# Key pages of a paged cache: one transfer of whole rows in place of two transfers of half rows

## The chip, the cores and the metric

The kernel runs on one core of a Trainium2 chip. The metric is the device time of one execution in microseconds; a lower one is better. The time before is the median of three runs.

## What is computed

One inference step of one decoder layer, for a prompt of 256 tokens and for 8 sample sequences with one new token each, all in f32. The part that the change touches is the attention of the 8 samples over their paged past of 2048 keys, 16 pages of 128 keys, found through a page table:

```
k_past = cache_k[l][page_table].reshape(bs, n_pages * PAGE_SIZE, N_HEADS, 2, HEAD_DIM)
v_past = cache_v[l][page_table].reshape(bs, n_pages * PAGE_SIZE, N_HEADS, V_DIM)

def diff_attention(q, k, v, q_pos, k_pos, rel_bias, lam):
    s = jnp.einsum('bqhjd,bkhjd->bhjqk', q, k) * (HEAD_DIM ** -0.5)
    ...
    p = jax.nn.softmax(s, axis=-1)
    p_diff = p[:, :, 0] - lam * p[:, :, 1]
    return jnp.einsum('bhqk,bkhe->bqhe', p_diff, v)
```

With 8 heads, two maps per head and 64 columns each, a key has 1024 values (4 KB); a page of 128 keys is 512 KB. Around it lie an input projection (`x @ w_in`), the same attention for the prompt, a complex diagonal state-space layer with GELU and a gate, two branch projections, an output projection, a gated MLP with a causal convolution, and two layer norms.

## The kernel before

The program is written out engine by engine, with semaphores. It has two parts. In the first, up to about 760 us, TensorE (PE) makes the 72 output tiles of the input projection and of the GLU as f32 products with weight tiles that stream through a ring (L708), and between them, at places counted in products (`z_groups` with its hooks `at`), does the small products of everything else. In the second part each weight tile is split by ACT (L1431) and DVE (L1899) into a high and a low part, and PE makes three products per tile (L1030, L1031, L1036).

The sample attention runs beside the projection, one sequence after the other: keys of sequence b+1 while the values of sequence b are used. For the keys:

- SyncE (SP) loads a page into `k_pages`, a ring of four pages. `load_keys` (L434) reads the page number from SBUF (`value_load`, L436), then for each half e of the row (512 of the 1024 columns) waits until that half of the slot is free and issues a transfer of 128 x 512 (L438, L439).
- GpSimd (POOL) multiplies a half in place by the query row that is broadcast to all partitions (`products`, L620; L627), after it waited for that half's transfer.
- VectorE (DVE) sums the products over the 64 columns of each map (`reduce_page`, L1728; L1735) into `score` and counts the half as free in `k_free`.

Pages are numbered n = 16 b + p, halves 2n + e; a half of the ring is used again every 8 halves, so half 2n + e waits for `k_free` at 2n + e - 7.

For the values, `load_values` (L442) waits until PE has used the page four before (`v_used`) and then calls `load_page` (L428), which reads the page number (L430) and issues one transfer of 128 x 1024 (L431). PE's product with it is `page_pv` (L681, L688).

All of these loads stand in one hand-written order on SP, which executes in order. For each of the seven turns of its loop (L471) it is

```
for what in ("K4", "Sk", "P14", "P15", "V0", "K5", "V1", "K6", "Sv", "V2", "K7", "V3", "K8", "Q", "V4", "K9",
             "V5", "K10", "V6", "K11", "V7", "V8", "K12", "V9", "K13", "V10", "K14", "V11", "K15", "V12",
             "N0", "N1", "V13", "N2", "N3"):
```

K is a key page of sequence i+1, N one of sequence i+2, V a value page of sequence i, P one of sequence i-1, Q the query row, Sk and Sv are stores of new keys and values. A load that waits holds back everything behind it.

POOL also executes in order, and it does a second task between the products: `fractions` (L616, L618), a step of the rotation tables of the state-space layer. In sequence 0 they stand before pages 4 and 8, later before pages 3, 5, 8 and 11. ACT makes their input (`turns`, L1213) and takes their output (`rotation`, L1220 to L1224), DVE uses the tables in `states` (L1679 to L1692), and PE waits for those states in `cx` (L797). DVE executes `states`, the reductions and the softmax of the prompt heads (`maxima`, `differences`) in one fixed order, given in the loop at L1797. The transfers of the weights are issued by ACT, on a queue of its own.

Of the kernel before, what the change touches and what calls it, by code (L numbers as in the profile page):

```python
# [27 lines left out]
PAGES = 16  # L28
POOL_PAGES = 160
KW = H * 2 * HD  # L30
# [50 lines left out]
def wait(eng, sem, value):  # L81

    if isinstance(value, int) and value <= 0:
        return
    eng.wait_ge(sem, value)
# [67 lines left out]
def build(nc, a, out, scratch):  # L153
    with ExitStack() as ctx:
        def sb(name, cols, dt=F32, rows=P):
            return ctx.enter_context(nc.sbuf_tensor(name, [rows, cols], dt))
# [18 lines left out]
        page_no = sb("page_numbers", B * PAGES, I32, rows=1)  # L175
# [3 lines left out]
        def overlay(*parts):  # L179
            with ExitStack() as stage:  # L180
                placed = [stage.enter_context(nc.sbuf_tensor(name, [P, cols], F32)) for name, cols in parts]
            return [t for t, (name, _) in zip(placed, parts) if not name.startswith("skip")]
# [31 lines left out]
        k_pages = work[:, 35288:39384]  # L214
# [57 lines left out]
        def half_page(n):  # L272
            return k_pages[:, n % 8 * KW // 2:(n % 8 + 1) * KW // 2]
# [19 lines left out]
        def sems(*names):  # L293
            return [sem(n) for n in names]
# [6 lines left out]
        k_in = sems(*(f"k_in{j}" for j in range(8)))  # L301
# [25 lines left out]
        kq_ready, k_free = sems("kq_ready", "k_pages_reduced")  # L327
# [37 lines left out]
        def _(sp):  # L365
# [56 lines left out]
            ck = a["cache_k"][0].rearrange("n p h j d -> n p (h j d)")  # L422
            cv = a["cache_v"][0].rearrange("n p h e -> n p (h e)")

            def cache_half(e):
                return ck[:, :, e * KW // 2:(e + 1) * KW // 2]

            def load_page(cache, ring4, arrived, b, p):  # L428
                n = PAGES * b + p
                at = sp.value_load(page_no[0:1, n:n + 1], min_val=0, max_val=POOL_PAGES - 1)  # L430
                sp.dma_start(page(ring4, n), cache[bass.ds(at, 1)].rearrange("o p k -> (o p) k")  # L431
                             ).then_inc(arrived[n % 4], 16)

            def load_keys(b, p):  # L434
                n = PAGES * b + p
                at = sp.value_load(page_no[0:1, n:n + 1], min_val=0, max_val=POOL_PAGES - 1)  # L436
                for e in range(2):
                    wait(sp, k_free, 2 * n + e - 7)  # L438
                    sp.dma_start(half_page(2 * n + e),  # L439
                                 cache_half(e)[bass.ds(at, 1)].rearrange("o p k -> (o p) k")).then_inc(k_in[(2 * n + e) % 8], 16)  # L440

            def load_values(b, p):  # L442
                wait(sp, v_used, PAGES * b + p - 3)
# [13 lines left out]
            for p in range(4):  # L457
                load_keys(0, p)
# [6 lines left out]
            for p in range(4, PAGES):  # L465
                load_keys(0, p)
            for p in range(4):
                load_values(0, p)
            for p in range(4):
                load_keys(1, p)  # L470
            for i in range(H - 1):  # L471
# [3 lines that stand above are left out]
                    kind, p = what[0], int(what[1:]) if what[1:].isdigit() else 0  # L475
# [117 lines left out]
        @block.gpsimd  # L593
        def _(pool):
            ch = Chain(pool, pool_c)
            ch.did(pool.memset(ident[:, :], 0.0))
            ch.wait()
            pool.affine_select(out=ident[:, :], in_=ident[:, :], compare_op=ALU.not_equal, fill=1.0, base=0,
                               pattern=[[-1, P]], channel_multiplier=1).then_inc(const_ready, 1)
            pool.memset(small[0:NB + 1, 32:32 + H], MASK).then_inc(rel_ready, 1)  # L600
            for tensor, value in ((ones[:, :], 1.0), (mean_w[:, :], 1.0 / D), (v_mean_w[:, :], 1.0 / P),
                                  (small[:, 4:5], PI / 2), (small[:, 5:6], EPS), (small[:, 6:7], 4 * EPS)):
                pool.memset(tensor, value).then_inc(const_ready, 1)

            times_i = score[0][:, 0:T].bitcast(I32)
            ch.did(pool.iota(times_i, pattern=[[1, T]], base=1, channel_multiplier=0))
            ch.wait()
            pool.tensor_copy(times, times_i).then_inc(times_ready, 1)
            pool.memset(b_pad[:, :], 0.0).then_inc(bpad_zero, 1)
            pool.memset(MT[:, :, 256:512], 0.0).then_inc(mt_zero, 1)  # L610

            def fractions(n):

                turns, whole_turns, part = (tab[n % 2][:, k * 256:(k + 1) * 256] for k in range(3))
                pool.wait_ge(tv_ready, n + 1)
                ch.did(pool.tensor_scalar(whole_turns, turns, 1.5 * 2 ** 23, -1.5 * 2 ** 23, ALU.add, ALU.add))  # L616
                ch.wait()
                pool.tensor_tensor(part, turns, whole_turns, ALU.subtract).then_inc(tf_ready, 1)  # L618

            def products(b, p):  # L620

                n = PAGES * b + p
                if p == 0:
                    pool.wait_ge(qb_in[b % 2], 16 * (b // 2 + 1))
                for e in range(2):
                    pool.wait_ge(k_in[(2 * n + e) % 8], 16 * (n // 4 + 1))
                    pool.tensor_tensor(half_page(2 * n + e), half_page(2 * n + e), q_b[b % 2][:, e * 512:(e + 1) * 512],  # L627
                                       ALU.mult).then_inc(kq_ready, 1)

            fractions(0)  # L630
            fractions(1)
            for p in range(PAGES):
                if p == 4:
                    fractions(2)
                if p == 8:
                    fractions(3)
                products(0, p)
            fractions(4)
            fractions(5)
            for i in range(H):  # L640
                for p in range(PAGES if i + 1 < B else 0):
                    if p == 3:
                        fractions(4 * i + 6)
                    if p == 5:
                        fractions(4 * i + 7)
                    if p == 8 and i + 2 < HT:
                        fractions(4 * i + 8)
                    if p == 11 and i + 2 < HT:
                        fractions(4 * i + 9)
                    products(i + 1, p)  # L650

            def centre(ln):

                pool.wait_ge(mean_copied, ln + 1)
                for g in (0, 1):
                    c3 = x3[:, 4 * g:4 * g + 4, :]
                    pool.tensor_tensor(c3, c3, mean_y.unsqueeze(1).to_broadcast([P, 4, N]), ALU.subtract  # L657
                                       ).then_inc(cent_ready, 1)

            centre(0)  # L660
            centre(1)
# [3 lines left out]
        def _(pe):  # L665
# [356 lines left out]
            def products(m, off, sums):  # L1022


                pe.wait_ge(wh_ready, m + 1)
                for dst, k0, highs, lows, start, _, ready in sums:
                    for k in range(len(highs)):
                        if ready is not None:
                            pe.wait_ge(*ready(k))
                        pe.matmul(dst[:, 0:N], weight(w_hi, off, k0 + k), highs[k], start=start and k == 0, stop=False)  # L1030
                        last = pe.matmul(dst[:, 0:N], weight(w_hi, off, k0 + k), lows[k], start=False, stop=False)  # L1031
                last.then_inc(wh_used, 1)
                pe.wait_ge(wl_ready, m + 1)
                for dst, k0, highs, _, _, stop, _ in sums:
                    for k in range(len(highs)):
                        last = pe.matmul(dst[:, 0:N], weight(w_lo, off, k0 + k), highs[k], start=False,  # L1036
                                         stop=stop and k == len(highs) - 1)
                last.then_inc(slot_done, 1)
# [1069 lines left out]
```

## Time and profile before

| | us |
|---|---|
| median of 3 runs | 1740.39 |
| lowest and highest | 1736.45, 1743.41 |
| profiled execution, its own time | 1737.55 |
| its span, first to last instruction | 1735.6 |
| busy: PE / DVE / ACT / POOL | 1660.1 / 1121.9 / 651.6 / 391.2 |
| mean clock granted to TensorE, share of full | 0.979 |
| read from HBM, written | 385.47 MB, 7.02 MB |

The sum of an engine's busy time says how full it is, not what ends the program. The stages have different limits: before 760 us transfers, POOL, DVE and PE hand work to each other, after it PE works nearly without a gap. In the rows below "idle" in brackets is the time in which the engine stood before the instruction, and behind the arrow is the work that released it. SPq is SyncE's own queue of instructions; its DMA rows show when a transfer is issued, and "DMA to landing" how long it took from there. L numbers are lines of the kernel before.

### The profile page before, as it was taken

The numbers are of one execution on the slowest core, as the hardware profiler recorded it, in microseconds if no ns is written. First come the engines' busy times: TensorE is split into PE (matmuls) and PEld (weight loads), VectorE is DVE, ScalarE is ACT, GpSimd is POOL, SyncE is SP. The second block draws the span as 40 slices with busy tenths as digits, with TensorE's granted clock in tenths as the row PEclk, the third lists the DMA queues.
The fourth block names the chain that finished last, engine by engine and source line by source line (L and its number), as shares of the span: only waits on it lengthen the run. The fifth ranks groups of instructions, "written<-read, shape, count | busy, mean of one in ns | idle before, by whom it ended". The sixth has DMA issues, their size and how long they took to land. (4 is left out here: it accounts for less than half of the span.)

```text
span 1735.6 us, 31618 instructions
## 1 busy us (share of the span) xinstructions
PE 1660.1 (96%) x11736; PEld 1473.4 (85%) x11736; DVE 1121.9 (65%) x1740; ACT 651.6 (38%) x986; POOL 391.2 (23%) x341
## 2 busy tenths in 40 slices
PE   7996999999999999989997999999999999999997
PEld 5884876666677667789997999999999999999996
DVE  1345487878878764567667767777777776555555
ACT  2021134434334322333335544444444444333333
POOL 1044576766866860000001000000000000000001
PEclk9898999999999999999998999999999999999998
DMA  9775899999999996776664557667667675766651
GB/s 224 169 228 169 274 325 368 361 376 384 362 379 378 367 344 213 225 195 177 183 182 121 158 160 209 176 174 195 163 184 188 169 190 143 211 175 181 178 163 51
DMA packets 502962, 393.63 MB, mean 227 GB/s; under 512 B 25439, under 2 KB 451316, under 8 KB 502548
## 3 DMA queue, kind: packets, MB, share of 16 engines
q1 hardware_dynamic: 419908, 325.07, 62.2%
q10 hardware_dynamic: 82944, 67.11, 12.3%
q8 instruction: 67, 1.10, 0.3%
q14 instruction: 43, 0.34, 0.1%
HBM read 385.47 MB, written 7.02 MB: 226 GB/s over the span
## 5 line engine op out<-in xcount | busy, mean ns | idle before, releaser
L708 PE MATMUL bank<-work,weight_ring 128*128 128x264 f32 x2176 | 522.5, 396 | 0.5 <-ACT work L1152 0.5
L1431 ACT ACTIVATE weights_hi<-weight_ring 128x2048 fp32r<-128x2048 f32 (+1 forms) x166 | 309.7, 1866 | 514.6 <-PE bank L1031 386.8
L708 PEld LDWEIGHTS bank<-work,weight_ring 128*128 128x128 f32 x2176 | 412.5, 194 | 94.8 <-issue 25.1
L1899 DVE TENSOR_TENSOR weights_lo<-weight_ring,weights_hi 128x2048 fp32r<-128x2048 f32 (+1 forms) x166 | 369.1, 2224 | 112.6 <-ACT weights_hi L1431 67.5
L627 POOL TENSOR_TENSOR work<-work 128x512 f32<-128x512 f32 x256 | 318.7, 1277 | 95.6 <-DMA work<-in_cache_k 73.9
L1030 PE MATMUL bank<-h_hi,weights_hi 128*128 128x264 f32 x1344 | 331.0, 284 | 0.0
L1031 PE MATMUL bank<-h_lo,weights_hi 128*128 128x264 f32 x1344 | 330.2, 284 | 0.0
L1030 PEld LDWEIGHTS bank<-h_hi,weights_hi 128*128 128x128 f32 x1344 | 253.2, 188 | 0.0
L1031 PEld LDWEIGHTS bank<-h_lo,weights_hi 128*128 128x128 f32 x1344 | 252.7, 188 | 0.0
L657 POOL TENSOR_TENSOR work<-work,ffn_scratch 128x1056 f32<-128x1056 f32 x4 | 9.5, 2407 | 1058.4 <-ACT ffn_scratch L1152 1058.4
L1735 DVE TENSOR_REDUCE work<-work 128x8 f32<-128x512 f32 x256 | 164.5, 677 | 47.8 <-POOL work L627 47.5
L1036 PE MATMUL bank<-h_hi,weights_lo 128*128 128x264 f32 x1344 | 176.5, 284 | 0.0
L1030 PE MATMUL bank<-hidden_hi,weights_hi 128*128 128x264 f32 x688 | 169.7, 284 | 1.8 <-DVE ffn_scratch L2027 1.8
L1031 PE MATMUL bank<-hidden_lo,weights_hi 128*128 128x264 f32 x688 | 169.3, 284 | 0.0
L1036 PEld LDWEIGHTS bank<-h_hi,weights_lo 128*128 128x128 f32 x1344 | 168.4, 188 | 0.0
L1152 ACT ACTIVATE work<-bank 128x256 f32<-128x256 f32 (+8 forms) x124 | 43.0, 357 | 305.2 <-PE bank L708 135.2
L1030 PEld LDWEIGHTS bank<-hidden_hi,weights_hi 128*128 128x128 f32 x688 | 129.5, 188 | 2.0 <-DVE ffn_scratch L2027 2.0
L1031 PEld LDWEIGHTS bank<-hidden_lo,weights_hi 128*128 128x128 f32 x688 | 129.4, 188 | 0.0
L2024 DVE SCALAR_TENSOR_TENSOR ffn_scratch<-bank,conv_and_ln_parameters,ffn_scratch 128x255 f32<-128x255 f32 x86 | 41.5, 483 | 128.0 <-ACT ffn_scratch L1152 128.0
L1036 PE MATMUL bank<-hidden_hi,weights_lo 128*128 128x264 f32 x688 | 91.3, 284 | 0.0
L1036 PEld LDWEIGHTS bank<-hidden_hi,weights_lo 128*128 128x128 f32 x688 | 86.7, 188 | 0.0
L688 PE MATMUL bank<-work 128*16 128x256 f32 x1024 | 71.0, 384 | 14.7 <-DMA work<-in_cache_v 13.9
(269 smaller groups left out, 1911.9 us busy)
## 6 DMA issues: line engine op xcount, KB each, us to landing
weight_ring<-in_w_up SPq DMA_DIRECT2D x86, 1024.0 KB, 5.7
work<-in_cache_k SPq DMA_DIRECT2D x256, 256.0 KB, 5.9
work<-in_cache_v SPq DMA_DIRECT2D x128, 512.0 KB, 6.1
weight_ring<-in_w_in ACTq DMA_DIRECT2D x60, 1024.0 KB, 11.5
weight_ring<-in_w_down SPq DMA_DIRECT2D x32, 1024.0 KB, 6.0
weight_ring<-in_w_out SPq DMA_DIRECT2D x16, 1024.0 KB, 6.0
weight_ring<-in_w_down SPq DMA_DIRECT2D x16, 704.0 KB, 4.9
weight_ring<-in_w_proj_attn SPq DMA_DIRECT2D x16, 512.0 KB, 4.2
```

Of the source, the lines that this page charges most:

```text
L627: pool.tensor_tensor(half_page(2 * n + e), half_page(2 * n + e), q_b[b % 2][:, e * 512:(e + 1) * 512], ALU.mult).then_inc(kq_ready, 1)
L657: pool.tensor_tensor(c3, c3, mean_y.unsqueeze(1).to_broadcast([P, 4, N]), ALU.subtract).then_inc(cent_ready, 1)
L688: last = pe.matmul(bank[5][32 * g:32 * g + 16, 0:2 * P], score[b % 3][:, p * 16:(p + 1) * 16], page(v_pages, n)[:, g * 2 * P:(g + 1) * 2 * ...
L708: last = pe.matmul(bank[(n + m) % 2][:, 0:N], chunk_weight(g, k - c * per, m), tiles[k], start=(k == 0), stop=(k == len(tiles) - 1))
L1030: pe.matmul(dst[:, 0:N], weight(w_hi, off, k0 + k), highs[k], start=start and k == 0, stop=False)
L1031: last = pe.matmul(dst[:, 0:N], weight(w_hi, off, k0 + k), lows[k], start=False, stop=False)
L1036: last = pe.matmul(dst[:, 0:N], weight(w_lo, off, k0 + k), highs[k], start=False, stop=stop and k == len(highs) - 1)
L1152: return act.activation(dst, src, ACT.Copy, scale=scale)
L1431: act.activation(w_hi[:, (j % 2) * KT * P:(j % 2) * KT * P + k_tiles * P].bitcast(F32R), slot3(j, 0, k_tiles).rearrange("p k m -> p (k m)" ...
L1735: dve.tensor_reduce(score[b % 3][:, p * 16 + 8 * e:p * 16 + 8 * e + 8], half_page(2 * n + e).rearrange("p (m d) -> p m d", d=HD), AX.X, AL ...
L1899: dve.tensor_tensor(w_lo[:, cols].bitcast(F32R), slot3(off % SLOTS, 0, k_tiles).rearrange("p k m -> p (k m)"), w_hi[:, cols], ALU.subtract ...
L2024: n1 = ch.did(dve.scalar_tensor_tensor(y[:, 1:T], ps[:, 0:T - 1], par(1), y[:, 1:T], ALU.mult, ALU.add))
```

## The change

`load_keys` now issues one transfer of 128 x 1024, by the same `load_page` as the values. It waits for both halves of the slot. The wait stands before the call, and so before the page number is read. POOL waits once per page, for the whole of it; its two products, DVE's two reductions and the two counts in `k_free` stay as they are. Of the eight semaphores `k_in` four are used.

```diff
@@ -422,9 +422,6 @@
             ck = a["cache_k"][0].rearrange("n p h j d -> n p (h j d)")
             cv = a["cache_v"][0].rearrange("n p h e -> n p (h e)")
 
-            def cache_half(e):
-                return ck[:, :, e * KW // 2:(e + 1) * KW // 2]
-
             def load_page(cache, ring4, arrived, b, p):
                 n = PAGES * b + p
                 at = sp.value_load(page_no[0:1, n:n + 1], min_val=0, max_val=POOL_PAGES - 1)
@@ -432,12 +429,8 @@
                              ).then_inc(arrived[n % 4], 16)
 
             def load_keys(b, p):
-                n = PAGES * b + p
-                at = sp.value_load(page_no[0:1, n:n + 1], min_val=0, max_val=POOL_PAGES - 1)
-                for e in range(2):
-                    wait(sp, k_free, 2 * n + e - 7)
-                    sp.dma_start(half_page(2 * n + e),
-                                 cache_half(e)[bass.ds(at, 1)].rearrange("o p k -> (o p) k")).then_inc(k_in[(2 * n + e) % 8], 16)
+                wait(sp, k_free, 2 * (PAGES * b + p) - 6)
+                load_page(ck, k_pages, k_in, b, p)
 
             def load_values(b, p):
                 wait(sp, v_used, PAGES * b + p - 3)
@@ -622,8 +615,8 @@
                 n = PAGES * b + p
                 if p == 0:
                     pool.wait_ge(qb_in[b % 2], 16 * (b // 2 + 1))
+                pool.wait_ge(k_in[n % 4], 16 * (n // 4 + 1))
                 for e in range(2):
-                    pool.wait_ge(k_in[(2 * n + e) % 8], 16 * (n // 4 + 1))
                     pool.tensor_tensor(half_page(2 * n + e), half_page(2 * n + e), q_b[b % 2][:, e * 512:(e + 1) * 512],
                                        ALU.mult).then_inc(kq_ready, 1)
```

Line numbers behind the first piece move up by 7 in the changed kernel; L427 and L428 there are L430 and L431 here.

On SP, at the key page "K4" of the second turn of the loop, the store behind it and the two value pages P14 and P15, the rows before are these (k_pages_reduced is `k_free`, v_pages_used is `v_used`; the ISA rows are register work):

```order
L436 TENSOR_LOAD page_numbers
L436 ISA x2
L439 ISA [waits k_pages_reduced]
L439 DMA work<-in_cache_k 128x512
L439 ISA [waits k_pages_reduced]
L439 DMA work<-in_cache_k 128x512
L452 DMA out_k_prompt<-work 128x2x128 [waits mail_read]
L430 TENSOR_LOAD page_numbers [waits v_pages_used]
L430 ISA x2
L431 ISA
L431 DMA work<-in_cache_v 128x1024
```

The same place in the changed kernel:

```order
L427 TENSOR_LOAD page_numbers [waits k_pages_reduced]
L427 ISA x2
L428 ISA
L428 DMA work<-in_cache_k 128x1024
L445 DMA out_k_prompt<-work 128x2x128 [waits mail_read]
L427 TENSOR_LOAD page_numbers [waits v_pages_used]
L427 ISA x2
L428 ISA
L428 DMA work<-in_cache_v 128x1024
```

One transfer and one wait are gone per key page, and the wait has moved from the register work behind the load of the page number to that load itself.

On POOL, at the first pages of sequence 0, before:

```order
L627 TENSOR_TENSOR work<-work 128x512 [waits k_in0,q_broadcast_in0]
L627 TENSOR_TENSOR work<-work 128x512 [waits k_in1]
L627 TENSOR_TENSOR work<-work 128x512 [waits k_in2]
L627 TENSOR_TENSOR work<-work 128x512 [waits k_in3]
L627 TENSOR_TENSOR work<-work 128x512 [waits k_in4]
```

And in the changed kernel:

```order
L620 TENSOR_TENSOR work<-work 128x512 [waits k_in0,q_broadcast_in0]
L620 TENSOR_TENSOR work<-work 128x512
L620 TENSOR_TENSOR work<-work 128x512 [waits k_in1]
L620 TENSOR_TENSOR work<-work 128x512
L620 TENSOR_TENSOR work<-work 128x512 [waits k_in2]
```

No product moved; each second one no longer waits for a transfer of its own.

## Rows read from the trace of the kernel before

**Rows 1.** The page, part 2: clock granted to TensorE in 40 slices, tenths of full.
```profile
PEclk9898999999999999999998999999999999999998
```

**Rows 2.** Stages: us, busy (count) of PE PEld DVE ACT POOL, PEclk, DMA, GB/s.
```profile
240.00:640.00 400.00, 383.74 (x2361) 273.25 (x2360) 319.94 (x533) 156.24 (x336) 292.06 (x249) 1.00 1.03 370
...
760.00:1735.00 975.00, 951.26 (x7714) 944.30 (x7713) 644.14 (x934) 415.64 (x479) 9.55 (x4) 0.99 0.63 170
```

**Rows 3.** Waits, whole run: who <- for whom: us in total, times, longest.
```profile
POOL work L627 <- DMA work<-in_cache_k: 73.9, 28, 15.3
...
PE bank L797 <- DVE conv_and_ln_parameters L1692: 16.2, 1, 16.2
...
PE bank L688 <- DMA work<-in_cache_v: 13.9, 15, 2.6
```

**Rows 4.** Timeline around the first long wait: start us, us, what, [idle <-releaser].
```profile
143.02 1.25 DVE L1735 TENSOR_REDUCE work<-work 128x8 f32<-128x512 f32 x2
...
143.86 0.92 SPq L439 DMA_DIRECT2D work<-in_cache_k  x2
...
146.25 2.46 DVE L1735 TENSOR_REDUCE work<-work 128x8 f32<-128x512 f32 x4
...
147.25 7.52 POOL L627 TENSOR_TENSOR work<-work 128x512 f32<-128x512 f32 x6 [15.32 <-DMA work<-in_cache_k]
...
164.98 1.91 PE L797 MATMUL bank<-conv_and_ln_parameters,work 128*32 128x256 f32 x4 [16.25 <-DVE conv_and_ln_parameters L1692]
```

**Rows 5.** Timeline of one turn of the loop (head 4).
```profile
437.07 1.07 POOL L616 TENSOR_SCALAR work<-work 128x256 f32<-128x256 f32 x1 [10.48 <-ACT work L1213]
...
448.12 19.93 POOL L627 TENSOR_TENSOR work<-work 128x512 f32<-128x512 f32 x16
...
467.11 1.25 DVE L1735 TENSOR_REDUCE work<-work 128x8 f32<-128x512 f32 x2
...
470.10 2.54 SPq L431 DMA_DIRECT2D work<-in_cache_v  x3
...
476.67 0.63 PE L688 MATMUL bank<-work 128*16 128x256 f32 x8 [0.94 <-DMA work<-in_cache_v]
```

**Rows 6.** PE's timeline, waits on value pages.
```profile
281.86 0.63 PE L688 MATMUL bank<-work 128*16 128x256 f32 x8 [1.45 <-DMA work<-in_cache_v]
283.11 1.05 PE L688 MATMUL bank<-work 128*16 128x256 f32 x8 [0.63 <-DMA work<-in_cache_v]
...
515.10 0.62 PE L688 MATMUL bank<-work 128*16 128x256 f32 x8 [1.42 <-DMA work<-in_cache_v]
...
605.94 0.63 PE L688 MATMUL bank<-work 128*16 128x256 f32 x8 [0.17 <-DMA work<-in_cache_v]
...
636.55 0.62 PE L688 MATMUL bank<-work 128*16 128x256 f32 x8 [1.21 <-DMA work<-in_cache_v]
```

**Rows 7.** Lines L430 and L431 (value pages), then L439 in 140:152 (half key pages).
```profile
L430 SPq TENSOR_LOAD <-page_numbers x128: 262/269/717, 177.0 to 712.2; - x128
...
L431 SPq DMA_DIRECT2D work<-in_cache_v x128: 332/333/615, 177.7 to 712.9; - x128
...
DMA to landing us min/median/max: 3.3/6.1/10.5
...
DMA to landing us min/median/max: 2.6/3.3/3.6
```

**Rows 8.** SP at page 79, L439 in 451.8:452.8, and POOL at page 31.
```profile
451.86 0.85 SPq L439 DMA_DIRECT2D work<-in_cache_k  x2
...
DMA to landing us min/median/max: 5.4/5.4/5.5
...
264.16 6.44 POOL L627 TENSOR_TENSOR work<-work 128x512 f32<-128x512 f32 x5 [0.45 <-DMA work<-in_cache_k]
```

**Rows 9.** Busy time in two short stretches, with PEclk; columns as above.
```profile
165.00:170.00 5.00, 5.00 (x11) 3.03 (x12) 5.00 (x10) 0.00 (x0) 4.15 (x4) 0.50 0.56 172
...
283.00:286.00 3.00, 2.89 (x12) 1.66 (x13) 2.90 (x6) 1.01 (x3) 1.58 (x2) 0.50 1.03 370
```


## The prediction

> **What bounds the kernel now.** I read the page first. TensorE's granted clock is 0.8 or more of full in every slice, mostly 0.9 or more [rows 1], so its time is work or waits, and only a little throttling. The table by stage adds that in 240 to 640 us PE works 383.7 of 400 us while the 16 DMA engines are full (share 1.03); after 760 us PE works 951 of 975 us and no key page is left [rows 2]. So what the change can move lies before 760 us, and there PE has little idle time. The waits name it [rows 3]: one wait of 16.2 us on the state chain (DVE L1692), and 13.9 us in 15 waits on value pages. PE never waits on a key page. GpSimd (POOL) does, for 73.9 us in 28 waits; SyncE (SP), which issues the loads, waits for DVE to free half pages before it. The question is which of these two lead to PE.
>
> The 16.2 us wait does. POOL reaches page 5 and stands until 147.25, since SP could issue that page only at 143.86, when DVE had reduced the halves of page 1. POOL then does six products, pages 5 to 7, in 7.52 us, and only behind them its fraction step L616. From it go the tables on ACT, the states on DVE and the product on PE (164.98 us) [rows 4]. Each us by which page 7's products end later is a us of PE.
>
> The value waits lead there too, by a loop of one turn per head, shown for one head [rows 5]: PE ends a tile, ACT evicts it and makes the next turns, POOL is released by them (437.07) and does 16 products in a row from 448.12, DVE reduces behind it up to page 79, and after its other work page 80 (467.11); SP, which had stood at the next key page, goes on through a store to value pages (470.10), and PE gets the second of them at 476.67 after a wait. PE waits at this place in each of six heads, from 2.1 us in the first (281.86 and 283.11) to 0.2 us in the last (605.94) [rows 6], and never runs into slack: the loop goes through PE and turns as slowly as its slowest way. The waits at page 9 of a sequence (such as 1.42 us at 515.10 [rows 6]) lie inside the same turn, so a longer one is taken back at the next place.
>
> **The change, part by part.** (1) The release. Before, the page number was read and the register work done ahead of the wait, and the transfer left 0.17 us after the reduction (DVE's first half of page 1 ends about 143.69, issue at 143.86 [rows 4]). Now the wait stands on the load of the page number, with all of that behind it. A value page already has this form: three of them in a row take 2.54 us [rows 5], 0.33 us of it the last issue itself [rows 7], so they start 1.10 us apart and 0.77 us lie between wait and issue; the load alone is 0.27 us [rows 7]. A key page therefore leaves 0.6 us later than its second half did, and 1.1 to 1.2 us later than its first. Behind it on SP stand the value pages, which leave 0.6 us later wherever SP had been waiting.
>
> The Trainium skill (DMA: Bandwidth & Descriptors, Latency and other measured facts) gives about 600 ns as the floor of such a load. The 0.27 us of the trace decides; with 0.6 the step would be 0.33 us longer in each of the eight places below, 2.6 us in all.
>
> (2) The landing. Halves landed in 2.6 to 3.6 us in the quiet stretch around 147 us; whole 512 KB value pages took 3.3 us at least, 6.1 in the median [rows 7]. In that quiet stretch I take 3.3 for a whole key page, the value page's shortest and the middle of the halves'; 3.0 and 4.0 are the ends. In the full stretch a pair of halves took 5.4 to 5.5 [rows 8], so beside a value page's 6.1 the size counts for a few tenths.
>
> (3) The start. Page 1's second reduction ended about 144.3, so page 5 is issued at 145.05 and lands at 148.35. Page 2 is reduced by 147.5 (two of the four from 146.25 [rows 4]): page 6 issued at 148.3, landed 151.6; its two products end at 154.1 (1.25 each), those of page 7 at 156.6, where they ended at 154.77. **+1.8 us**, between 1.2 and 2.5. The clock stands at 0.50 (1.2 GHz) for the first 5 us after PE resumed [rows 9]. A later start may shorten or lengthen that tail by half of a few us; I take 0, bounds -1 and +2.
>
> (4) The loop, in six heads. The key page that stands ahead of the value pages leaves 0.6 us later: **+3.6 us**. Inside the turn POOL can also wait for pages 14 and 15. At head 4 it took page 79 at 448.12 + 8 x 1.246 = 458.1; the halves, issued at 451.86 and 452.38, landed in 5.4 to 5.5 us, the last at 457.9 [rows 8]. Slack 0.2 against a page 0.3 to 0.6 later: +0.4. At head 1 POOL already waited 0.45 for page 31 [rows 8], so there the full 0.9 counts. Nearly all other rows of POOL in the turn run on without such a wait. Mean 0.5, bounds 0 and 1: **+3.0 us**, 0 to 6. The wait of 1.21 us at 636.55, in the last turn [rows 6], has a key page ahead of its value page on SP: **+0.6 us**.
>
> (5) What is saved. One DMA issue per page (the starts of the pair at 451.86 are 0.85 - 0.33 = 0.52 us apart [rows 8]). Where SP was waiting this saves nothing; where it was not, value pages leave 0.5 us earlier, but those have 1 to 8 us of room. 128 transfers fewer on full engines: bounds 0 and -3 us (at most 0.2 us for each of two landings in the loop, in seven turns), and I take **-1 us**, near the end at 0, since a landing hardly depends on size. POOL's wait count falls by one in two, which has no price: its products follow at 1.25 us in either form. The reductions and their releases stay.
>
> Sum: 1.8 + 3.6 + 3.0 + 0.6 - 1 = **+8 us**. The profiled execution took 1737.55 us, so 1745.6, say **1746 us**. The median of the three runs is 1740.39, 2.8 us above that execution, and they spread over 7 us, so 1748 by the median; about 0.5% (8.7 us) is what a measurement can tell from no change here. The forecast lies just inside it.
>
> **The rivals.**
> *Hidden.* Only the start pays, because the loop has some room that the trace doesn't show (DVE or ACT may wait somewhere in the turn for work that is not on it): +2 us, 1740. For it: the turn's waits are short, 0.2 to 2.1 us [rows 6]. Against it: they come back in six heads of six.
>
> *The key ring becomes the bound (slower).* The place is POOL's run over pages 8 to 15. A slot now turns in two products 2.49, the last reduction 0.68, release 0.77 and a landing L, 3.94 + L; POOL needs 9.97 us for four pages. It decides from L = 6.0 us on, and the median of a value page is 6.1 [rows 7]. At L = 7.0 each four pages cost 1 us, two fours per turn and six turns 12 us more: 1758. Against it: landings are longest when the queue also holds pages that can leave earlier now.
>
> *The clock.* After the two waits at 281.86 and 283.11 (1.45 and 0.63 us) the clock stood at 0.50 for 283 to 286 us [rows 6, 9], a loss of 1.5 us. If longer waits bring this on at the other five turns: +7.5 us, 1753. Against it: the single wait of 1.42 us at 515.10 did not.
>
> *Larger transfers pay (faster).* If whole rows shorten the landings so much that the value pages come in time, at most all 13.9 us of these waits go: 1724, and half of it would be 1731. For it: DMA is full in this stretch. Against it: the waits come from when SP issues, not from bandwidth alone; at 470.10 the value pages leave 1.7 us after the reduction of page 80 (467.11 + 1.25) let SP go on [rows 5], and there the bandwidth has no say.
>
> For that rival speaks the Trainium skill (DMA: Bandwidth & Descriptors, Bandwidth), which wants transfers batched and measures 138 GB/s at 64 KB against 341 at 1 MB. No run here compares sizes alone; the two landings above speak against much of it.
>
> **How the numbers follow.** Forecast (+5 to +11 us) 0.50, hidden 0.20, key ring 0.12, clock 0.10, larger transfers 0.08. Of the forecast's 0.50 about 0.15 lies above 8.7 us; with the ring and most of the clock case slower has 0.36. Faster has half of the last case, 0.04; the rest is 0.60. The range leaves out the gain and the far ends of ring and clock: 1739 to 1759 us.
>
> **What would show it.** Right: the first wait of PE on L1692 grows from 16.2 to about 18 us; key issues come 0.77 us after the reduction; the value waits grow from 13.9 us to some 17 to 21; POOL's waits on keys grow in the loop; all after 760 us stays. Wrong: value waits below 13.9 us, a first wait that is not longer, POOL idle before most pages (the ring), or new stretches at clock 0.50.

## The result, and the profile after

| | before | after |
|---|---|---|
| median of 17 runs, us | 1739.8 | 1745.72 |
| lowest and highest, us | 1733.49, 1743.41 | 1740.59, 1751.69 (one more at 3306.83) |
| span of the profiled execution, us | 1735.6 | 1742.0 |
| clock granted to TensorE | 0.979 | 0.98 |
| POOL's waits on key pages | 73.9 in 28 | 81.6 in 44 |
| PE's waits on value pages | 13.9 in 15 | 19.9 in 19 |
| PE's wait on the state chain | 16.2 | 18.4 |

The ratio is 1.0041, with an interval of 1.0028 to 1.0054: slower by 0.4%, a difference of 5.9 us in the medians. One execution of 3306.83 us stands apart and is left out of the ratio. Runs of the changed kernel beside later experiments gave 1.0054 [1.0033 to 1.0074] again.

The page of the changed kernel, its clock, the queue and the issues:

```profile
PEclk9997999999999999999998999999999999999998
...
q1 hardware_dynamic: 401476, 325.07, 62.0%
...
work<-in_cache_k SPq DMA_DIRECT2D x128, 512.0 KB, 6.1
work<-in_cache_v SPq DMA_DIRECT2D x128, 512.0 KB, 6.2
```

The clock row is that of before but for two slices near the start [rows 1]. Half the transfers of keys, twice as large, land 6.1 us after their issue in the median. On the page of the kernel before, the same two rows are these:

```profile
q1 hardware_dynamic: 419908, 325.07, 62.2%
...
work<-in_cache_k SPq DMA_DIRECT2D x256, 256.0 KB, 5.9
```

So the bytes are the same, the time that they take on the 16 DMA engines is the same (62.0 against 62.2%), and one whole row lands about as late after its issue as one half did.

The stages of the changed kernel (columns as in rows 2):

```profile
240.00:640.00 400.00, 378.99 (x2317) 270.07 (x2316) 316.36 (x521) 156.17 (x336) 289.16 (x246) 1.00 1.01 364
760.00:1742.00 982.00, 956.54 (x7765) 950.07 (x7763) 648.91 (x941) 417.43 (x480) 9.54 (x4) 0.99 0.64 171
```

In 240 to 640 us PE is busy for 4.75 us less than before, with the DMA share still at full. The waits (as in rows 3):

```profile
POOL work L620 <- DMA work<-in_cache_k: 81.6, 44, 16.5
...
PE bank L681 <- DMA work<-in_cache_v: 19.9, 19, 1.7
PE bank L790 <- DVE conv_and_ln_parameters L1685: 18.4, 1, 18.4
```

PE's two waits grew by 2.2 and 6.0 us. The timeline around the first of them, to be read against [rows 4]:

```profile
141.34 1.25 DVE L1728 TENSOR_REDUCE work<-work 128x8 f32<-128x512 f32 x2
...
143.35 5.16 SPq L428 DMA_DIRECT2D work<-in_cache_k  x3
...
146.69 2.48 POOL L620 TENSOR_TENSOR work<-work 128x512 f32<-128x512 f32 x2 [16.53 <-DMA work<-in_cache_k]
...
165.44 1.91 PE L790 MATMUL bank<-conv_and_ln_parameters,work 128*32 128x256 f32 x4 [18.39 <-DVE conv_and_ln_parameters L1685]
```

DVE ends the second half of page 1 at 142.59, the transfer of page 5 leaves at 143.35, 0.76 us later, and POOL begins 3.34 us after that. Between pages POOL now stands too (the piece of 1.14 us before page 6 is in its 44 waits); before, all six products ran in one piece.

Where the time went follows from the start of the same instruction in both executions. PE's first products on the last of the 16 value pages, at the ends of the first three turns and of the sixth; the last row is page 7 of the seventh sequence, inside the last turn:

```profile
283.74 0.62 PE L681 MATMUL bank<-work 128*16 128x256 f32 x8 [1.10 <-DMA work<-in_cache_v]
...
349.44 0.62 PE L681 MATMUL bank<-work 128*16 128x256 f32 x8 [1.33 <-DMA work<-in_cache_v]
...
415.47 0.84 PE L681 MATMUL bank<-work 128*16 128x256 f32 x8 [1.26 <-DMA work<-in_cache_v]
...
612.14 0.62 PE L681 MATMUL bank<-work 128*16 128x256 f32 x8 [1.07 <-DMA work<-in_cache_v]
...
642.51 0.63 PE L681 MATMUL bank<-work 128*16 128x256 f32 x8 [0.96 <-DMA work<-in_cache_v]
```

- Up to the small products of `cx` that start at 106.88 us (108.56 before) the changed kernel is 1.68 us ahead. Nothing of the change acts there; a stretch at half clock was shorter in this execution (last section).
- From there to the end of the first long wait: 165.44 against 164.98, so 2.14 us lost.
- To the last page of the first turn: 283.74 against 283.11, 0.17 us more.
- From there to the last page of the sixth: 328.40 against 322.83 us (605.94 - 283.11 [rows 6]), 5.57 us lost.
- On to page 7 in the last turn, 642.51: 30.37 against 30.61 us, nothing lost; and the second part begins at 752.84 against 746.79, the end comes at 1742.0 against 1735.6. Nothing happens behind 760 us.

### The profile page after: what moved, and what is told of

The parts are those of the page before. It is cut to its first block and busy times, and to the rows that moved or that the text cites. A ratio compares the mean times of both kernels' runs of the same rounds, so it can differ in the third digit from the quotient of the medians.

```text
span 1742.0 us, 31234 instructions
## 1 busy us (share of the span) xinstructions
PE 1657.2 (95%) x11736; PEld 1471.8 (84%) x11736; DVE 1124.6 (65%) x1740; ACT 651.3 (37%) x986; POOL 391.8 (22%) x341
## 5 line engine op out<-in xcount | busy, mean ns | idle before, releaser
L620 POOL TENSOR_TENSOR work<-work 128x512 f32<-128x512 f32 x256 | 319.3, 1276 | 103.1 <-DMA work<-in_cache_k 81.6
L681 PE MATMUL bank<-work 128*16 128x256 f32 x1024 | 70.6, 383 | 20.5 <-DMA work<-in_cache_v 19.9
```

Of the source, the lines that this page charges most:

```text
L681: last = pe.matmul(bank[5][32 * g:32 * g + 16, 0:2 * P], score[b % 3][:, p * 16:(p + 1) * 16], page(v_pages, n)[:, g * 2 * P:(g + 1) * 2 * ...
```

## The experiments

Ratios are to the kernel before, run on the same chip in the same series. e1, e2, e3 and e4 shared one chip, e0, e5, e7 and e9 a second, e1 again, e7 again and e8 a third.

**The page number read ahead of the wait, whole rows kept (e1).**

```diff
 def load_keys(b, p):
-    wait(sp, k_free, 2 * (PAGES * b + p) - 6)
-    load_page(ck, k_pages, k_in, b, p)
+    n = PAGES * b + p
+    at = sp.value_load(page_no[0:1, n:n + 1], min_val=0, max_val=POOL_PAGES - 1)
+    wait(sp, k_free, 2 * n - 6)
+    sp.dma_start(page(k_pages, n), ck[bass.ds(at, 1)].rearrange("o p k -> (o p) k")
+                 ).then_inc(k_in[n % 4], 16)
```

> The changed kernel, with the page number read before the wait for the slot and only the transfer behind it. My theory prices the register load behind the wait at 0.6 us in each of the two release steps of the start and in each turn of the loop, 3.6 of the 6.1 us that the loop lost and 0.6 of the start. Expected: key issues 0.17 us after the reduction again; the first wait of PE about 17.8 us instead of 18.4; value waits near 16 us instead of 19.9; the time 3 to 4 us below the changed kernel, 1741.5 to 1743 (ratio to before 1.001 to 1.002). Rival one, the whole transfer and POOL's wait for all of it carry the cost: the time stays at 1744 to 1746. Rival two, the landing of larger transfers: the same, 1744 to 1746.

Measured: 1736.42 us, ratio 0.9994 [0.9976 to 1.0011], and a second time 1736.81, 0.9992 [0.9974 to 1.001]. The whole loss is gone, more than was expected.

> The changed kernel with the page number read before the key wait, again, to narrow its interval. By the theory that the load behind the wait is the whole cost of the loop, only the start's 1.3 us remain and SP saves an issue per page: ratio 0.999 to 1.001. If it lies at 1.002 or above, whole transfers cost something by themselves.

Its timeline:

```profile
140.74 1.25 DVE L1731 TENSOR_REDUCE work<-work 128x8 f32<-128x512 f32 x2
142.18 4.75 SPq L435 DMA_DIRECT2D work<-in_cache_k  x3
...
145.77 2.48 POOL L623 TENSOR_TENSOR work<-work 128x512 f32<-128x512 f32 x2 [15.82 <-DMA work<-in_cache_k]
```

Its waits:

```profile
POOL work L623 <- DMA work<-in_cache_k: 72.7, 34, 15.8
...
PE bank L684 <- DMA work<-in_cache_v: 14.3, 15, 2.1
PE bank L793 <- DVE conv_and_ln_parameters L1688: 17.6, 1, 17.6
```

From the end of the reduction (141.99) to the issue it is 0.19 us, not 0.76. The value waits are back at 14.3, against 13.9 before and 19.9 after. The first wait stays 1.4 us above that of before: in the quiet stretch the late release of the first half and the landing of the whole row remain, and e2 below has 0.6 of the 1.4 us.

**Halves kept, the first half released as late as the second (e2).**

```diff
 for e in range(2):
-    wait(sp, k_free, 2 * n + e - 7)
+    wait(sp, k_free, 2 * n - 6)
```

> The kernel before, with one constant changed: the first half of a key page waits, like the second, until both halves of the slot are free. Two transfers of half rows, the number read first, POOL waiting per half. Both halves leave 0.6 us and 0.5 us later than before, and the value pages behind them 0.5 us later. Expected by my theory (what counts is when SP goes on behind the key page, and when the last half lands): start +0.6 to +1.1 us, loop +0.5 us a turn, so +3 to +4.5 us, 1743 to 1744.5 (ratio 1.002 to 1.0025). Rival, only whole pages and larger transfers cost: ratio 1.000, 1740. Against the run with the number first it tells what one transfer in place of two is worth with the same wait.

Measured: 1741.16 us, 1.0016 [0.9996 to 1.0036]. The middle is a little below what was expected, and no change lies in the interval too, so alone it decides nothing. Beside e1 it does more. Both read the number first and wait for the same count, and they differ in halves against whole rows only: 0.9994 and 0.9992 against 1.0016, about 4 us for the whole rows. Single runs of the two overlap; the means of the twelve runs of each on one chip differ by 4.2 us, with an interval of 1 to 7. In e2's trace PE's first wait is 16.8 us and the value waits are 18.7, in e1's 17.6 and 14.3: whole rows cost a little in the start and give more back in the loop.

**Two more loads behind the wait (e9).** Their results are not used.

```diff
 def load_keys(b, p):
     wait(sp, k_free, 2 * (PAGES * b + p) - 6)
+    n = PAGES * b + p
+    for _ in range(2):
+        sp.value_load(page_no[0:1, n:n + 1], min_val=0, max_val=POOL_PAGES - 1)
     load_page(ck, k_pages, k_in, b, p)
```

> The changed kernel with two more loads of the page number (results unused) between the wait for the slot and the transfer of a key page: the suspected cost tripled, by about 1.1 to 1.2 us a page. If the load behind the wait is what the change costs, through the first stall once and through the turn of each head, the time rises by another 9 to 14 us over the changed kernel (start +1.1, six turns +1.2 to +1.9 each, the last turn +1), ratio to before 1.009 to 1.012; PE's first wait 19.3 to 19.6 us, value waits 27 us or more. Rival, the transfers or POOL's whole-page wait carry the cost and SP has room: under 3 us more, ratio below 1.006.

Measured: 1765.08 us, 1.0158 [1.0138 to 1.0177], beside 1745.17 for the changed kernel in the same series (e0). That is more than expected.

> The changed kernel as it is, on the same chip as the others of this call, so that they can be compared with it directly. Expected by every theory: ratio to before 1.003 to 1.005.

In e9 the reduction of page 1 ends at 142.44 and the issue comes 1.85 us later; the timeline, from POOL's row at 460.06 on in the turn of head 4:

```profile
144.29 5.75 SPq L428 DMA_DIRECT2D work<-in_cache_k  x3
...
460.06 2.49 POOL L623 TENSOR_TENSOR work<-work 128x512 f32<-128x512 f32 x2 [0.41 <-DMA work<-in_cache_k]
462.90 2.50 POOL L623 TENSOR_TENSOR work<-work 128x512 f32<-128x512 f32 x2 [0.34 <-DMA work<-in_cache_k]
466.66 5.26 POOL L623 TENSOR_TENSOR work<-work 128x512 f32<-128x512 f32 x4 [1.26 <-DMA work<-in_cache_k]
474.38 2.50 POOL L623 TENSOR_TENSOR work<-work 128x512 f32<-128x512 f32 x2 [2.46 <-DMA work<-in_cache_k]
```

Its waits:

```profile
POOL work L623 <- DMA work<-in_cache_k: 124.3, 73, 16.4
...
PE bank L684 <- DMA work<-in_cache_v: 29.6, 23, 3.6
```

POOL stands before 73 of the 128 pages, where it stood before 44 in the changed kernel: here the ring of keys has become a bound, as in the rival of that name. In the changed kernel it hardly has. The same run of pages there:

```profile
452.75 12.58 POOL L620 TENSOR_TENSOR work<-work 128x512 f32<-128x512 f32 x10
...
465.49 2.67 POOL L620 TENSOR_TENSOR work<-work 128x512 f32<-128x512 f32 x2 [0.17 <-DMA work<-in_cache_k]
...
468.96 2.49 POOL L620 TENSOR_TENSOR work<-work 128x512 f32<-128x512 f32 x2 [0.80 <-DMA work<-in_cache_k]
471.66 2.50 POOL L620 TENSOR_TENSOR work<-work 128x512 f32<-128x512 f32 x2 [0.21 <-DMA work<-in_cache_k]
```

Ten of the sixteen products run without a stop, then three short waits, where before all sixteen ran in one piece [rows 5]. With e1 there are three points: issue 0.19, 0.76 and 1.85 us behind the reduction, ratio 0.9993, 1.0048 (the middle of 1.0041 and 1.0054) and 1.0158. The first step costs 9.6 us for 0.57 us, the second 19 us for 1.09 us: 17 us of time for each us of delay, in both.

That is not the price of the delay alone. The mean granted clock over all runs is 0.980 in e1, 0.979 in the changed kernel and 0.974 in e9. The share not granted, times the span, is 35, 38 and 45 us. By this estimate, which counts every such us as lost, up to 3 us of the first step and up to 8 us of the second are clock. Without them each us of delay costs 10 to 12 us.

**Value pages ahead of the key pages at two places on SP (e3), and the same in the kernel before (e4).**

```diff
-                for what in ("K4", "Sk", "P14", "P15", "V0", ...
+                for what in ("P14", "P15", "K4", "Sk", "V0", ...
...
-                             ... "V7", "V8", "K12", "V9", "K13", ...
+                             ... "V7", "V8", "V9", "K12", "K13", ...
```

> The changed kernel with another order on SP: value pages 14 and 15 stand ahead of the key page 4 of the next sequence, value page 9 ahead of key page 12. These value pages no longer stand behind a key page that waits for DVE. By my theory the value waits of PE at these places (about 17 of 19.9 us) go, and with them the loop: the time falls by 12 to 17 us to 1729 to 1734. Only the start's 2 us of the change then remain against the same order of the kernel before. Rival, POOL or the key ring bounds the turn: PE waits for ACT, DVE or other value pages instead, and the time falls by under 5 us.

> The kernel before with the same new order on SP (value pages 14 and 15 ahead of key page 4, value page 9 ahead of key page 12). My theory: some 10 of the 13.9 us of value waits go, the time falls by 8 to 11 us to 1729 to 1732, and the changed kernel in this order is only about 2 us slower than this one. Rival, the change costs its 6 us on another way than through the value pages: the two stay 6 us apart.

Measured: e3 1724.81 us, 0.9924 [0.9902 to 0.9946]; e4 1726.3, 0.9929 [0.9904 to 0.9955]. Both gain more than expected, and the two can't be told apart. The value waits of e3, then of e4:

```profile
PE bank L681 <- DMA work<-in_cache_v: 2.8, 5, 0.9
```

```profile
PE bank L688 <- DMA work<-in_cache_v: 7.6, 6, 2.6
```

In this order the changed kernel is no longer measurably the slower one. So its loss in the loop went through the value pages that stood behind a waiting key page. The gain of the new order (12 us on the kernel before, 20 us on the changed one) shows also what this order costs before any change.

**The fraction step of sequence 0 before page 5 instead of page 8 (e5, on the changed kernel).**

```diff
-                if p == 8:
+                if p == 5:
                     fractions(3)
```

> The changed kernel with one step moved on POOL: the fraction step that stood before the products of page 8 of sequence 0 now stands before those of page 5, where POOL waits for a transfer anyway. If the first wait of PE (18.4 us) is the chain page 5 landed, six products, fraction step, tables, states, it shrinks to 6 to 8 us, since DVE can begin the states at its last reduction (about 149 us) and not at 160; the time falls by 9 to 12 us against the changed kernel to 1733 to 1736 (a shorter stretch at the lower clock may add 1 to 3 us). Rival, the states wait for something else (ACT's table or DVE's reductions of page 4): under 3 us.

Measured: 1735.18 us, 0.9989 [0.9976 to 1.0002], 10 us below e0. The wait and what ends it:

```profile
146.15 2.48 POOL L620 TENSOR_TENSOR work<-work 128x512 f32<-128x512 f32 x2 [8.31 <-DMA work<-in_cache_k]
...
153.06 1.92 PE L790 MATMUL bank<-conv_and_ln_parameters,work 128*32 128x256 f32 x4 [6.61 <-DVE conv_and_ln_parameters L1685]
```

The step now fills a part of POOL's own wait for page 5, and PE resumes at 153.06 instead of 165.44. This shows the first chain as the prediction read it: key pages 5 to 7 lead to PE's longest wait through POOL's fixed order. By the estimate used above for e9, up to 4 of the 10 us are clock.

**All together, with the change (e7) and without it (e8).** e7 is the changed kernel with the edits of e1, e3 and e5, and values too read their number ahead of the wait; e8 is the kernel before with the order of e3, the step of e5 and the same for values.

> The changed kernel with all that the theory says helps: number read before the wait for keys and for values, value pages 14, 15 and 9 ahead of the key pages that wait, fraction step before page 5. The new SP order alone gave 1724.8 on the changed kernel. Adding the other two: 9 to 12 us from the first stall, 1 to 3 us from the remaining value waits and the 0.6 us of release. Expected 1711 to 1715 (ratio 0.984 to 0.987), faster than both kernels. Rival, the gains overlap and another wait takes their place: 1718 or more.

> The kernel before with everything of the run with all together except the change itself: halves as before, new order on SP, fraction step before page 5, number read before the wait for values too. It tells whether whole-row transfers are worth anything once nothing waits behind them. My theory: 128 fewer issues on SP let the value pages that still wait (page 5 and page 13 of a sequence, 7.6 us in the half-row kernel with the new order against 2.8 us in the whole-row one) leave earlier, so this kernel is 2 to 6 us slower than the whole-row one: 1711 to 1715, ratio 0.985 to 0.988. Rival, whole rows are worth nothing or cost the first half's delay: this kernel is equal or faster, ratio 0.982 to 0.984.

> The run with all together, again, on the same chip as its half-row counterpart for a direct comparison. Expected by every theory: ratio 0.982 to 0.986.

Measured: e7 1708.96 us, 0.9836 [0.9813 to 0.9859], and again 1713.06, 0.9856 [0.9827 to 0.9886]; e8 1718.21, 0.9886 [0.9857 to 0.9915]. e8 lies 3 us above what was expected. On one chip e7 is 5.2 us faster than e8, and of its six runs one reaches into the range of e8's six (1717.35 against a lowest of 1716.14); the intervals overlap a little. PE's value waits are 7.5 us in e8's trace and 2.2 in that of e7 again. So whole rows are worth some 0.3% in this order, with the number read first. e7 is 1.4 to 1.6% faster than the kernel before, and 2.1% faster than the changed kernel beside it (e0).

## Why the prediction came out right, step by step

The forecast was 1746 us and the median 1745.72; the case that it named, a late release that reaches PE by two ways, is the one that the runs show. The steps, against the two traces:

- *The release* (0.77 us after the reduction): 0.76. *The landing* (3.3 us in the quiet stretch): POOL begins after 3.34.
- *The start*, +1.8 us: 2.14. Behind page 5 POOL waited 1.14 us more, for page 6.
- *The loop*, +3.6 + 3.0 - 1, so +5.6 us: 0.17 + 5.57 = 5.74 up to the last page of the sixth turn.
- *The last turn*, +0.6 us: not there. The wait is 0.96 us, less than the 1.21 of before [rows 6], and the stretch up to it takes 0.24 us less.
- The gross sum is 8.1 us; the span grew by 6.4, since this execution came to 106.88 us 1.7 us early. The forecast, +8 on one execution, was a little above the difference of the medians, 5.9 us, and of the 7.1 us that the ratio makes of 1739.8.

**The mechanism and the sum are right, but two parts behind the sum were off, and cancel; that it hit the median within 1 us is luck.** e1 splits the change in two:

- The load behind the wait (e1 to after): 0.0048 to 0.0061, 8 to 11 us. The prediction had 3.6 + 0.6 us for it ahead of the value pages, some 0.6 us in the start, and a share of the 3.0 us for pages 14 and 15, so 5 to 8 us.
- All the rest, whole rows with the number read first (before to e1): ratios of 0.9994 and 0.9992, some 1 us gained, which can't be told from 0. The prediction had what is left of its sum, 0 to 3 us lost.

e2 splits the rest once more: 0.0016 or 2.8 us from before to e2, which its interval doesn't tell from 0, and 4.0 us back from e2 to e1. These 4 us do not measure the term *What is saved* (-1, with a bound of -3). In e2 the second half is issued some 0.5 us behind the first, and both behind the release; a whole row leaves with the first. In the kernel before, where SP is waiting, the second half leaves at its own release: for page 5 at 144.45 (143.86 + 0.92 - 0.33 [rows 4, 7]), 0.18 us after the second reduction (143.02 + 1.25 [rows 4]), and the whole row of e1 leaves 0.19 us after it. So against the kernel before, "where SP was waiting this saves nothing" stands, and e1 gains back for the larger part what e2 had lost. In 240 to 640 us the median from issue to landing is 6.3 us for e1's whole rows and 6.0 for e2's halves, so in e1 a page is complete 0.2 us earlier and SP goes on 0.5 us earlier. That this is the way of the 4 us is argued; no run took it away alone.

The term of the load was sized as eight places (the start, six turns, the last turn) and a mean of 0.5 us at a second place in each of six. The 10 to 12 us per us measured without the clock are near that; the 17 with it are what two places in each of seven turns and the start would make, 15. So what was too small is the clock, which the prediction took at 0 and for the start alone, or the second place. The second can be POOL's waits for pages 14 and 15 (bound 6 us, taken at 3), or PE's waits inside a turn, at page 9 for most, which the prediction took as paid back at the turn's end. In the two traces the 6.0 us more of value waits are 4.2 at the ends of the six turns (5.1 to 9.3 us) and 1.8 inside them (7.6 to 9.4); the wait at page 9 of the fourth sequence that PE uses is one of these, first before, then after:

```profile
450.29 0.62 PE L688 MATMUL bank<-work 128*16 128x256 f32 x8 [0.79 <-DMA work<-in_cache_v]
```

```profile
455.64 0.62 PE L681 MATMUL bank<-work 128*16 128x256 f32 x8 [1.52 <-DMA work<-in_cache_v]
```

So they were not paid back in full. e3 moved the value pages of both places in one run, so how much of the cost belongs to each stays open.

The rivals. *Hidden*: fell, the value waits were longer in each of the first five turns, by 0.5 to 2.1 us, and 0.2 us shorter in the sixth and in the last. *The key ring*: not yet as forecast, but it is what happens with two more loads; POOL's waits went from 28 to 44 and, in e9, to 73. Its point of decision was right in kind: landings of 6.3 us in the full stretch lie just above the 6.0 that were named, and POOL waits 0.2 to 0.8 us before three pages of the turn. *The clock*: in the two profiled executions the loop has one short stretch below full before [rows 9] and one after, so nothing of the difference between these two. Over all runs it is a small part: the mean granted clock was 0.9784 in 16 runs of the changed kernel and 0.9793 in 57 of the kernel before, by estimate 1 to 2 us of the 6. The stretch after:

```profile
415.00:420.00 5.00, 4.53 (x19) 3.15 (x19) 4.90 (x9) 2.32 (x4) 3.49 (x5) 0.66 1.00 383
```

In e9, with waits up to 3.6 us, there are four such stretches (at 384, 459, 487 and 521 us, clock 0.53 to 0.66 over 5 us), so it is a part of what e9 cost. *Larger transfers pay*: not through bandwidth, the queue's share stayed at 62.0%. Whole rows paid 4 us beside e2 and 5 us beside e8, but beside the kernel before itself e1 shows no gain that can be told from 0, and the change as it was made spends 8 to 11 us on the load.

The Trainium skill (DMA: Bandwidth & Descriptors, Bandwidth) wants transfers batched and measures, for transfers issued from GpSimd, 138 GB/s at 64 KB against 341 at 1 MB. The full stretch moved 370 GB/s with halves [rows 2] and 364 with whole rows, so from 256 KB up no gain of that kind is left here. The Trainium skill (DMA: Bandwidth & Descriptors, Latency and other measured facts) gives about 600 ns as the floor for a load of a register. That is not borne out for the load alone, though the load and the register work behind it together moved the issue by 0.57 us. 128 loads of key page numbers and 128 of value pages in the changed kernel took

```profile
L427 SPq TENSOR_LOAD <-page_numbers x256: 262/269/624, 78.4 to 718.1; - x128
```

## What to carry to other kernels

On an engine that issues in order, everything that does not need the wait belongs ahead of it: reading an index behind the wait instead of ahead of it cost 0.57 us per page and 8 to 11 us in all, about twice what merging the transfers gave at its best (5 us, e8 to e7). Order loads on such a queue by who releases them, and never put one with a late releaser ahead of one whose slot is already free; here that alone was worth 12 to 20 us. When a small step lies on the way to the bounding engine, put it where its own engine waits anyway (10 us), and count a delay once for each place of the loop that it passes, not once per turn. Ask too what the longer waits do to the granted clock.

## What the runs showed of the hardware that was not expected

The size of a transfer had little effect on the time from issue to landing, full queue or not. In 240 to 640 us the medians are 6.2 us for 256 KB (before) and 6.4 for 512 KB (the changed kernel's key pages). In the quiet stretch around 145 us halves landed in 2.6 to 3.6 us (medians 3.3 before, 2.9 in e2) and whole rows in 3.2 to 4.4 (medians 3.3 in the changed kernel, 3.5 in e1).

Two executions differ before the change can act. In 43 to 54 us TensorE, busy all the time, had a mean clock of 0.54 in the kernel before and 0.69 in the changed one:

```profile
43.00:54.00 11.00, 11.00 (x50) 10.38 (x50) 0.00 (x0) 0.61 (x2) 0.00 (x0) 0.54 0.68 194
```

```profile
43.00:54.00 11.00, 11.00 (x57) 9.65 (x57) 0.00 (x0) 0.61 (x2) 0.00 (x0) 0.69 0.69 192
```

The level of 0.50 (1.2 GHz) lasted some 10 us in one and 7 us in the other, and that is the 1.7 us by which the changed kernel was ahead. The profiled execution of the changed kernel in e0 took 1735.6 us with a mean clock of 0.984, against a median of 1745.17 in the same series. A single profiled execution of each kernel could have shown no difference at all, or twice the true one; at 0.4% only the medians of many runs tell, and the trace tells where.
